# Merging the two directions' decay arguments before the exponential in a bidirectional state-space scan

## What is computed

```python
def segsum_exp(a):                      # a: (..., 128), one chunk of one head
    cs = jnp.cumsum(a, axis=-1)
    diff = cs[..., :, None] - cs[..., None, :]
    tri = jnp.asarray(np.tril(np.ones((T, T), dtype=bool)))
    return jnp.where(tri, jnp.exp(jnp.where(tri, diff, 0.0)), 0.0)

def ssd_chunked(x, dt, A, Bm, Cm):      # called once forward, once on flipped inputs
    CB = jnp.einsum('bclgn,bcsgn->bcgls', Cc, Bc)
    Wd = CB[:, :, :, None] * segsum_exp(adt)
    y_diag = jnp.einsum('bcgrls,bcsgrp->bclgrp', Wd, xdt)
    ...
    return (y_diag + y_off).reshape(b, l, H, P)
```

## Time and profile before

| | before |
|---|---|
| median of 3 runs | 2540.72 us |
| span of the profiled execution, first to last instruction | 2537.0 us |
| PE busy | 2479.5 us (98%) |
| PE weight loads busy | 2019.3 us (80%) |
| DVE busy | 1471.2 us (58%) |
| ACT busy | 1165.1 us (46%) |
| POOL busy | 160.2 us (6%) |
| chain that ended last | PE 81%, DVE 10%, ACT 6%, issue 3% |
| mean granted TensorE clock | 0.997 |

### The profile page before, as it was taken

How to read it: one execution, slowest core, us unless ns; L and a number is a source line. 1 busy time by engine, 2 the same in 40 slices (tenths; PEclk the granted TensorE clock), 3 DMA queues, 4 the chain that set the end, 5 groups by cost and what they waited for, 6 DMA issues and landing times.

```text
span 2537.0 us, 36072 instructions
## 1 busy us (share of the span) xinstructions
PE 2479.5 (98%) x14504; PEld 2019.3 (80%) x14504; DVE 1471.2 (58%) x2374; ACT 1165.1 (46%) x2099; POOL 160.2 (6%) x156
## 2 busy tenths in 40 slices
PE   9999999999999999999999999999999999999998
PEld 6888778888776678888877888888877877788886
DVE  6665554433656564344378898786677556543343
ACT  5354352322456644233257666665455444432232
POOL 2110110000200010000001111111000010100001
PEclk9999999999999999999999999999999999999999
DMA  5222234544322223333322222222322233233322
GB/s 154 76 60 76 59 101 114 129 110 113 100 80 82 67 80 94 100 93 98 100 74 85 67 67 69 74 78 73 95 67 67 93 122 102 75 108 100 93 98 75
DMA packets 197093, 226.50 MB, mean 89 GB/s; under 512 B 7552, under 2 KB 132768, under 8 KB 196672
## 3 DMA queue, kind: packets, MB, share of 16 engines
q1 hardware_dynamic: 196928, 224.21, 30.2%
HBM read 214.22 MB, written 9.44 MB: 88 GB/s over the span
## 4 chain that ended last, share of the span: by engine, by line
PE 81%; DVE 10%; ACT 6%; issue 3%; DMA 0%; POOL 0%; DVEq 0%; SPq 0%; ACTq 0%; POOLq 0%
PE bank L1986 22%; PE bank L1988 22%; PE bank L1987 22%; PE bank L1992 2%; DVE CV L2720 2%; PE bank L1994 1%; PE bank L1993 1%; DVE wlo L2484 1%; PE bank L2005 1%; ACT whi L2263 1%; PE bank L2195 1%; PE bank L2203 1%; ACT XAh L2272 1%; PE bank L2216 1%; DVE h L2518 1%
## 5 line engine op out<-in xcount | busy, mean ns | idle before, releaser
L2484 DVE TENSOR_TENSOR wlo<-raw,whi 128x1024 fp32r<-128x1024 f32 x389 | 489.7, 1265 | 629.8 <-ACT whi L2263 627.5
L2263 ACT ACTIVATE whi<-raw 128x1024 fp32r<-128x1024 f32 x389 | 408.9, 1058 | 580.9 <-PE bank L1988 569.2
L1986 PE MATMUL bank<-XAh,whi 128*128 128x512 f32 x1552 | 615.8, 397 | 10.7 <-issue 4.3
L1988 PE MATMUL bank<-XAh,wlo 128*128 128x512 f32 x1552 | 602.1, 388 | 0.0
L1987 PE MATMUL bank<-XAl,whi 128*128 128x512 f32 x1552 | 602.0, 388 | 0.0
L1986 PEld LDWEIGHTS bank<-XAh,whi 128*128 128x128 f32 x1552 | 291.7, 188 | 83.8 <-issue 16.2
L1988 PEld LDWEIGHTS bank<-XAh,wlo 128*128 128x128 f32 x1552 | 291.8, 188 | 61.2
L1987 PEld LDWEIGHTS bank<-XAl,whi 128*128 128x128 f32 x1552 | 292.1, 188 | 57.8 <-issue 1.0
L1986 PE MATMUL bank<-XBh,whi 128*128 128x512 f32 (+1 forms) x840 | 331.2, 394 | 1.8 <-DVE XBl L2490 1.7
L1988 PE MATMUL bank<-XBh,wlo 128*128 128x512 f32 (+1 forms) x840 | 323.9, 386 | 0.0
L1987 PE MATMUL bank<-XBl,whi 128*128 128x512 f32 (+1 forms) x840 | 323.9, 386 | 0.0
(11 more groups left out here) (346 smaller groups left out, 3296.0 us busy)
## 6 DMA issues: line engine op xcount, KB each, us to landing
raw<-in_w_in SPq DMA_DIRECT2D x77, 512.0 KB, 3.9
raw<-in_up SPq DMA_DIRECT2D x64, 512.0 KB, 3.7
raw<-in_down SPq DMA_DIRECT2D x64, 512.0 KB, 3.7
raw<-in_a_w_in SPq DMA_DIRECT2D x32, 512.0 KB, 4.2
raw<-in_w_up SPq DMA_DIRECT2D x32, 512.0 KB, 3.7
raw<-in_w_down SPq DMA_DIRECT2D x32, 512.0 KB, 3.6
raw<-in_w_kv SPq DMA_DIRECT2D x16, 512.0 KB, 3.6
raw<-in_w_ssd_branch SPq DMA_DIRECT2D x16, 512.0 KB, 3.5
```

The costliest lines, as they stand in the source:

```text
L1986: pe.matmul(out, wh[:, w, c], xh[:, x, r], start=st, stop=False)
L1988: m = pe.matmul(out, wl[:, w, c], xh[:, x, r], start=False, stop=en)
L2263: act.activation(s.hi, s.raw, ACT.Copy).then_inc(s.whi[0], 1)
L2484: dve.tensor_tensor(s.lo, s.raw, s.hi.bitcast(F32), ALU.subtract).then_inc(s.wlo[0], 1)
```

## The change

Before, ACT takes the exponential of both directions (128x512 each), and DVE then merges the results. Now DVE merges the arguments under the same mask (the same `copy_predicated` on the same 128x512 operands), ACT takes one 128x512 exponential of the merged tile, and DVE multiplies it by `CB`. So a head goes from ACT to DVE to ACT to DVE, where it went from ACT to DVE. The step `sc_exp` keeps the 8 Relus and loses its exponentials; `sc_merge` (DVE) and `sc_pow` (ACT) are new; `sc_w` keeps the multiplication alone, and waits for the exponential where it waited for DVE's own merge.

```diff
                     s = add("sc_arg", banks=bs, rowT=rowT, hd=4 * g + r_, rows=ready["rows"], arg=[sig("sc.arg"), sig("sc.arg")])
-                    s = add("sc_exp", banks=bs, E=E, hd=4 * g + r_, cols=ready["cols"], arg=s.arg, below=[sig("sc.below"), sig("sc.below")], exp=[sig("sc.exp"), sig("sc.exp")])
+                    s = add("sc_exp", banks=bs, E=E, hd=4 * g + r_, cols=ready["cols"], arg=s.arg, below=[sig("sc.below"), sig("sc.below")])
                     for b, v in zip(bs, s.below):
                         b.free(v)
+                    s = add("sc_merge", E=E, below=s.below, merged=sig("sc.merged"))
+                    yield
+                    s = add("sc_pow", E=E, merged=s.merged, exp=sig("sc.exp"))
                     yield
                     s = add("sc_w", E=E, CB=CB.t, exp=s.exp, cb=after[g].cb, w_done=sig("sc.w"))
...
                 m.then_inc(s.below[d][0], 1)
-            for d in range(2):
-                on.wait_ge(*s.below[d])
-                act.activation(s.E.t[:, d, :], s.E.t[:, d, :], ACT.Exp, scale=-1.0, bias=cap).then_inc(s.exp[d][0], 1)
+        elif k == "sc_pow":
+            on.wait_ge(*s.merged)
+            act.activation(s.E.t[:, 0, :], s.E.t[:, 0, :], ACT.Exp, scale=-1.0, bias=K.cap[:, 0:1]).then_inc(s.exp[0], 1)
...
+        elif k == "sc_merge":
+            for d in range(2):
+                on.wait_ge(*s.below[d])
+            dve.copy_predicated(c4(s.E.t[:, 0, :]), K.late[:, :].bitcast(U32).unsqueeze(1).to_broadcast([P, 4, P]), c4(s.E.t[:, 1, :])).then_inc(s.merged[0], 1)
         elif k == "sc_w":
-            for d in range(2):
-                on.wait_ge(*s.exp[d])
-            dve.copy_predicated(c4(s.E.t[:, 0, :]), K.late[:, :].bitcast(U32).unsqueeze(1).to_broadcast([P, 4, P]), c4(s.E.t[:, 1, :])).then_inc(*on.link())
-            on.linked()
+            on.wait_ge(*s.exp)
             on.wait_ge(*s.cb)
             dve.tensor_tensor(s.E.t[:, 0, :], s.E.t[:, 0, :], s.CB, ALU.mult).then_inc(s.w_done[0], 1)
```

More of the change, by code:

```diff
@@ L2402, in act_program @@
             on.room(s.E)
-            cap = K.cap[:, 0:1]
             on.wait_ge(*s.cols)
```

## The result

The changed kernel takes 2552.29 us (median of 4 runs, 2551.96 to 2552.6) against 2541.09 us for the kernel before (4 runs, 2540.25 to 2541.94). The ratio is 1.0045, with a 95% interval from 1.0033 to 1.0057: slower by 11.2 us. The profiled execution took 2552.39 us with a span of 2550.1 us; the span before was 2537.0 us. (In the executions listed for all kernels of this case the whole time lies 1.8 to 3.9 us over the span, so that spans of single executions compare to about 2 us.)

A forecast was written before the change was run, and what follows sets the result against it. The prediction took DVE to set the pace for heads 1 to 13 and PE for heads 14 to 32. Terms 1.2 + 5.1 + 3.4 + 1.7 = 11.4 us on 2540.7 gave 2552.1 us, range 2543 to 2562.

The forecast's parts named there:

- The price of a late head: Between merge and multiplication: each head where DVE is late costs DVE 0.9 us, with nothing else able to run.
- 1370 to 1411 us: Heads 1 to 3: 0.3 us for the first two and 0.9 for the third, 1.2 us; head 4 costs 0.
- 1438 to 1498: Heads 5 to 9, all late: four at 0.9 us and head 6 at 1.5, together 5.1 us.
- 1498 to 1546: Heads 10 to 13: head 10 1.1 us, three at 0.9, less 0.4 into a gap, together 3.4 us.
- After 1546: PE leads and slack takes the stalls, except at heads 17, 21 and 25: together 1.7 us.
- (c): Rival, lockstep: ACT never runs ahead, 5 us more, and PE's clock may drop, up to 1.7 us each; 2560; chance 0.20.
- PE's wait at head 8: At head 8's output: PE's wait of 1.50 us becomes about 4 as stalls of heads 5 to 8 arrive together.
- The walk at head 6: Head 6: multiplication ends 1.0 us sooner, then late `whi` and POOL delay `wlo`, leaving DVE 2.4 us behind.
- B: Time DVE comes behind the Relus' end; change -0.35 us near zero, zero at 0.4, +0.9 from 1.3 on.
- (a): Rival: DVE's idle time takes most stalls, leaving one per group on PE's path, some 3 us; 2544; chance 0.13.
- (b): Rival: the POOL collision is not met again behind heads 6 and 10, 2 x 1.2 us less; 2549.7; chance 0.12.
- (d): Rival: not slower, as the shorter chain decides and stalls fall into DVE's idle time, -3.4 us; 2537.3; chance 0.05.

The follow-up runs named there:

- the part with groups 0 to 2: Changed order for groups 0 to 2 (heads 1 to 12) alone, old order for the rest: 2550.15 us, 9.6 us slower than the kernel before.
- a run of its own: Kernel before with both exponentials, ACT waiting for DVE's merge at heads 6 and 10 alone: 2541.6 us, 0.8 us slower.
- the doubled merge: Kernel before with DVE's merge done twice, the second writing the same values: 2554.4 us, 13.8 us slower.
- saving the exponential: Kernel before with the second direction's exponential left out and no handover added: 2538.1 us, 2.4 us faster.
- holding ACT: Kernel before with both exponentials, ACT then waiting for DVE's merge at every head: 2543.51 us, 2.9 us slower.
- the halves: Changed kernel with merge, exponential and multiplication in two halves of 256 columns: 2546.11 us, 5.3 us slower than the kernel before.

## Why the prediction was right, and where not

The forecast was 11.4 us slower, 2552.1 us; measured were 11.2 and 2552.29. That two numbers meet so closely is partly luck, as the steps show.

- **What bounds.** That DVE sets the pace for heads 1 to 13 and PE after them was right: the part with groups 0 to 2 costs 9.6 us, the other 2.5.
- **The price of a late head**, 0.9 us, was 0.79 of idle time where there was 0.03 before, so 0.76. The step put the exponential at 0.774 us as in the pair, where alone it takes 0.724, and the two handovers at 0.14, where 0.79 - 0.72 = 0.07 us is left for both. The 0.10 that was read at head 17 holds for a merge behind ACT (0.10 at seven heads of the changed kernel too), not for the multiplication (0.03). The sum at 0.76 per late head would have been 1 to 1.5 us lower.
- **1370 to 1411 us:** 1.2 forecast. The outputs show 0.5 (head 4 against head 1), but DVE lost 1.8 (0.10 us late before head 1, 1.90 before head 5), and PE met it at 1443 us. Head 4, costed at nothing, cost the 0.9: the `wlo` behind head 3 met POOL (2.50 us instead of 1.22, begun at 1409.38), which the walk had only behind heads 6 and 10, and so used up the time that DVE had in hand before head 4. **1438 to 1498:** 5.1 forecast, 6.73 - 1.90 = 4.8, with 0.7 of it from the clock. **1498 to 1546:** 3.4 forecast, 3.9, with 0.8 from the clock. **After 1546:** 1.7 forecast, 1.7, 0.6 at each of the three heads named.
- **Where the luck lies.** The sum had too much at each late head (1 to 1.5 us in all) and at heads 6 and 10 (0.5 us, next point but one), and too little at head 4 (0.9) and for the clock (1.4 in the profiled execution, nothing in the sum). These nearly cancel. The lower clock stands only in rival (c).
- **PE's wait at head 8** was to become about 4 us, and is 2.59: the stalls of heads 5 to 7 did not all arrive there, as PE had already waited 0.77 us at head 7 and another 1.34 us for a `wlo` between the two heads.
- **The walk at head 6** was right in kind: merge and multiplication without POOL, then `wlo` late by `whi` and beside POOL's work (2.19 us of waiting, 2.11 us of run time). The expectation drawn from it for a run of its own, 2 to 3 us at heads 6 and 10, failed: 0.8, not to be told from zero. The expectation misread the sum: the 1.5 and 1.1 us that it had for these heads hold DVE's own gaps of 0.9, which that run leaves out, so that 2.6 - 1.8 = 0.8 us was left for it, the 0.8 that came out. In the changed kernel's trace DVE comes 1.16 us later at head 6 and 0.92 at head 10, with 0.76 of each the gap. The page "SBUF — State Buffer" of the Trainium skill, section "Who interferes with whom", says that a DVE instruction with two SBUF inputs contends with a GpSimd instruction that reads SBUF; the trace agrees, as `wlo`, with its two inputs in SBUF, took 2.11 us beside POOL at head 6 once the merge had left that time.
- **What is saved** was counted only inside the price (B under 0.4). Alone it is 2.4 us, a little over the 1 to 2 that I expected for it.
- **The rivals.** (a), slack takes most: ruled out by the doubled merge (13.8 us). (b), no collision: the collision took place. (c), lockstep: half right. ACT's idle time before the exponential is 64 us, where I had said some 40, so ACT is in lockstep indeed; but holding it costs 2.9 us in all, part of which the forecast already had at heads 6 and 10, where the rival asked for 5 more. The granted clock did drop behind PE's waits at two places, as the rival said, and it cost 0.7 and 0.8 us there, not 1.7, since DVE felt only what was left of PE's delay when it came to the convolution. (d) fell with the result.

The account in the end, from runs: saving the exponential -2.4, holding ACT +2.9 (0.8 to 5.3), and the rest, 11.2 + 2.4 - 2.9 = 10.7 us, for DVE's gap of 0.79 us at the 13 or so heads where DVE or its output is waited for. From the rows of the one profiled execution: gaps at heads 3 to 13, 11 x 0.75 = 8.3 us (heads 1 and 2 pay theirs out of the earlier merge), and 1.7 at heads 17, 21 and 25, so 10.0; the clock 1.4; the rest of heads 6 and 10 0.6. That is 12.0 of the 12.2 us by which DVE, and behind it PE, fell back in the scan; it is an estimate from one execution, and the medians differ by 11.2. Neither account need add up exactly, since the parts lie at the same places; that the gap is the largest of them is shown by the doubled merge and by the halves, and both accounts give 10 to 11 us for it.

## What to carry to other kernels

Count what an engine pays for a handover, not only what instructions it loses. An exponential moved between two instructions of an in-order engine puts its whole run time on that engine's path, and makes the engine that computes it give up its lead. Here 20 us of saved work were worth 2.4 us and the gaps of 0.79 us cost more than four times that. And where a second engine has the path, a lower clock on PE isn't free for that reason: look whether the path comes back through PE's results, as here at the next convolution. Ask which of the two engines comes late at the merge: with DVE late, as here, the change lengthened the path; the case with ACT late was not tried.

## What the runs showed of the hardware

One 128x512 exponential takes 0.724 us alone, and each of a pair back to back 0.774, while the pair together needs 1.39; one of 128x1024 takes 1.152. The way from DVE's merge through ACT's exponential back to DVE adds 0.07 us to the exponential's own time, both handovers together. A merge beside POOL took 2.0 us and without it 0.73; when the merge left that time, the next DVE instruction with two SBUF inputs took 2.11 us instead of 1.2. After PE's longer waits the granted clock fell in the changed kernel, busy times and clock in 10 us slices:

```profile
1470.00:1480.00 10.00, 6.07 (x65) 5.30 (x64) 8.94 (x16) 4.60 (x13) 1.32 (x1) 0.88 0.18 54
1480.00:1490.00 10.00, 10.00 (x76) 9.81 (x76) 7.62 (x11) 4.75 (x14) 0.70 (x1) 0.95 0.19 52
...
1520.00:1530.00 10.00, 7.59 (x100) 6.19 (x99) 8.92 (x17) 5.85 (x14) 0.27 (x1) 0.94 0.20 54
1530.00:1540.00 10.00, 10.00 (x72) 9.84 (x72) 8.60 (x12) 3.82 (x11) 1.75 (x1) 0.89 0.19 53
```

Part of each slice ran at 1.2 instead of 2.4 GHz. PE had waited 2.59 us for head 8's multiplication ahead of the first drop and 1.98 us for head 12's ahead of the second. The drop doesn't follow from the wait alone: in the run with groups 0 to 2 changed PE waited 2.59 us at the same place, was busy for the same 6.07 us of the slice from 1470 to 1480 us, and the granted clock there was 1.00. The slower matmuls were on the path: DVE's next convolution had to wait for them through ACT's tap, 0.58 us at head 9 and 0.70 at head 13.
